# A hybrid attention, recurrence and MLP kernel: thirty input chunks of block 2 by seven products, outputs parked in DRAM

## What is computed

```
h = rms_norm(x, norm_mix)
xa, ga, q, f, v, g, m_a, m_b = split(h @ w_in, 8)          # 1024 x 8192
y_a = rg_lru(conv4(xa), w_r, w_i, lam) * gelu(ga)           # scan over tokens
y_b = rms_norm(hgrn2(silu(q), 1 - f_gate, log f_gate, v)) * silu(g)
y   = sigmoid(m_a) * y_a + sigmoid(m_b) * y_b
x   = x + y @ w_out
x   = x + square(relu(rms_norm(x) @ w_up)) @ w_down         # 4096 wide
return rms_norm(x)
```

## Time and profile before

| | us |
|---|---|
| runs (3) | 3150.05, 3146.99, 3151.70; median 3150.05 |
| profiled execution | 3149.78 |
| its span | 3148.0 |
| busy: PE, DVE, ACT, POOL | 2957.5, 1878.6, 1111.7, 1030.2 |
| granted TensorE clock, mean | 0.976 |

### The profile page before, as it was taken

The page is one execution under the profiler, slowest core; times in us unless marked ns, Lnnn a source line. Parts: engine busy times, 40 slices in busy tenths (PEclk is TensorE's granted clock), DMA queues, the critical chain, the costliest instruction groups (busy, mean ns, idle before and its releaser), DMA issues.

```text
span 3148.0 us, 48352 instructions
## 1 busy us (share of the span) xinstructions
PE 2957.5 (94%) x19622; PEld 1847.6 (59%) x19842; DVE 1878.6 (60%) x3077; ACT 1111.7 (35%) x1972; POOL 1030.2 (33%) x1000
## 2 busy tenths in 40 slices
PE   7979998999979988999999999999999989999998
PEld 7529876884439667864565655655655434444443
DVE  2475797773489996644465465365364474545455
ACT  2353455663356745643231232132232221111111
POOL 1401365000512681012522322323221334545452
PEclk9998999999989999999999999999999999999999
DMA  7323142002201341021211111110112101111111
GB/s 248 133 69 108 58 148 88 15 22 96 96 14 42 110 142 32 12 85 67 82 41 41 41 41 41 54 41 28 54 41 81 41 27 54 54 54 54 54 54 74
DMA packets 49165, 207.13 MB, mean 66 GB/s; under 512 B 4488, under 2 KB 9776, under 8 KB 32304
## 3 DMA queue, kind: packets, MB, share of 16 engines
q1 hardware_dynamic: 42288, 195.63, 18.0%
q10 hardware_dynamic: 6656, 8.39, 0.9%
HBM read 187.22 MB, written 16.79 MB: 65 GB/s over the span
## 4 chain that ended last, share of the span: by engine, by line
PE 75%; DVE 18%; ACT 4%; issue 3%; DMA 0%; SPq 0%; DVEq 0%; ACTq 0%
PE big L276 16%; PE big L277 16%; PE big L275 15%; PE banks L275 5%; PE banks L276 5%; PE banks L277 5%; PE banks L1046 3%; DVE arena L1800 2%; DVE arena L1787 2%; PE banks L917 2%; DVE arena L2034 1%; PE big L591 1%; PE banks L591 1%; DVE arena L2200 1%; DVE arena L2014 1%
## 5 line engine op out<-in xcount | busy, mean ns | idle before, releaser
L561 POOL TENSOR_TENSOR w_lo<-stage,w_hi 128x512 bf16<-128x512 f32 x464 | 588.1, 1299 | 380.6 <-ACT w_hi L1245 380.0
L554 POOL CAST w_hi<-stage 128x512 bf16<-128x512 f32 x376 | 251.1, 709 | 1383.0 <-PE big L277 1188.2
L276 PE MATMUL big<-ht_lo,w_hi 128*128 128x512 bf16 x1161 | 440.0, 379 | 4.3 <-DVE ht_lo L1685 1.8
L277 PE MATMUL big<-ht_hi,w_lo 128*128 128x512 bf16 x1163 | 440.8, 379 | 1.2
L275 PE MATMUL big<-ht_hi,w_hi 128*128 128x512 bf16 x1137 | 430.9, 379 | 11.2 <-DVE arena L2061 6.5
L275 PE MATMUL big<-w_hi,ht_hi 128*128 128x256 bf16 (+1 forms) x1272 | 379.8, 299 | 12.9 <-DVE arena L1618 4.7
L276 PE MATMUL big<-w_lo,ht_hi 128*128 128x256 bf16 (+1 forms) x1274 | 380.3, 298 | 4.0 <-issue 3.7
L277 PE MATMUL big<-w_hi,ht_lo 128*128 128x256 bf16 (+1 forms) x1276 | 380.7, 298 | 0.3
L1800 DVE TENSOR_SCALAR_CACHE_REDUCE arena<-arena,smalli 128x512 bf16<-128x512 f32 (+5 forms) x268 | 206.7, 827 | 2.4
L275 PEld LDWEIGHTS big<-ht_hi,w_hi 128*128 128x128 bf16 x1184 | 117.5, 99 | 148.0 <-issue 11.5
L277 PEld LDWEIGHTS big<-ht_hi,w_lo 128*128 128x128 bf16 x1184 | 115.8, 98 | 139.7
(11 more groups left out here) (361 smaller groups left out, 6598.9 us busy)
## 6 DMA issues: line engine op xcount, KB each, us to landing
stage<-in_w SPq DMA_DIRECT2D x130, 1024.0 KB, 4.8
arena<-in_w_ada SPq DMA_DIRECT2D x48, 512.0 KB, 4.2
arena<-in_x SPq DMA_DIRECT2D x16, 512.0 KB, 7.6
xs<-arena SPq DMA_DIRECT2D x16, 512.0 KB, 2.6
arena<-xs SPq DMA_DIRECT2D x16, 512.0 KB, 8.3
gt<-arena ACTq DMA_DIRECT2D x16, 256.0 KB, 2.5
arena<-gt ACTq DMA_DIRECT2D x16, 256.0 KB, 2.6
out_x<-arena SPq DMA_DIRECT2D x8, 512.0 KB, 2.6
```

Source lines behind the costliest of these rows:

```text
L276: pe.matmul(out, ah, bl, start=False, stop=False)
L277: return pe.matmul(out, al, bh, start=False, stop=stop)
L554: pool.tensor_copy(w_hi[:, n % RING, c0:c1], stage[:, n % RAW_RING, c0:c1]).then_inc(s_w_hi_split, mark(s_w_hi_split, n, q))
L561: ins = pool.tensor_tensor(w_lo[:, n % RING, c0:c1], stage[:, n % RAW_RING, c0:c1], w_hi[:, n % RING, c0:c1], ALU.subtract)
```

## The change

**Block 2 input chunks.** 30 of the 32 (all but xa0 and f0, and not ri) go by seven products of 512 x 512 by 128 quarters. p1, p6, p7 and p4 are added up in one PSUM bank, p5 and p3 in another, p2 in a third. ACT copies the partial sums out after p1, p6 and p5 and applies the function after p4; DVE has three adds. PE waits before p6 for ACT's copy of p1, before p7 for that of p6, before p3 for that of p5, and before p4 for DVE's c22. Chunk order is xa, f, q, v, ri, ga, mb, gg, ma, and one step of the recurrence follows every seventh of 28 groups (four steps in a chunk, four in ri as before).
**Their weights.** POOL makes four sums and seven low parts, ACT seven high parts, for the chunk after the one that PE is in. A chunk has seven parts of 512 columns; two such slots and one for ri take the ring.
**Token sums** of block 2 (`sums_2`) are made by DVE and ACT at its start.
**Outputs** of bands 0 to 2 are stored in DRAM (`y2`), and loaded again by ACT (`y2_load`) after p4 of ma3; `first_two` waits for all six. SP loads six tiles of x after the same product, two after y2_f.
**MLP**: up2 is an ordinary chunk; three adds in place of seven, with partial sums in PSUM and ACT copies; `token_sums(1)` goes beside the first `add_down`, and behind the copy of up1 on ACT.
**Block 1**: the order of `choose` and the convolution on DVE, and the ada pieces spread inside `conv_in`.

```diff
-B_CHUNKS = ["xa", "f", "q", "v", "ri", "ga", "ma", "gg", "mb"]
+B_CHUNKS = ["xa", "f", "q", "v", "ri", "ga", "mb", "gg", "ma"]
-STRASSEN = range(2, 16)
+STRASSEN = range(3, 16)
+SEVEN = [n for n, (l, c) in enumerate(CHUNKS) if l == 2 and c[:-1] in B_CHUNKS and c[:-1] != "ri" and c not in ("xa0", "f0")]
+PRODUCTS = (("p1", 0, "b11", "u"), ("p2", 1, "b21", "p2"), ("p6", 4, "t2", "u"), ("p5", 3, "t1", "p5"), ("p7", 5, "t3", "u"), ("p3", 6, "b22", "p5"), ("p4", 2, "t4", "u"))
...
+        IN_CHUNK = {"v": hsteps[0:4], "ga": hsteps[8:12], "mb": hsteps[12:16], "gg": hsteps[16:20], "ma": hsteps[20:24]}
...
-                if n == CHUNK_AT[(2, "up1")]:
+                if n == CHUNK_AT[(2, "o3")]:
+                    sp.wait_ge(s_gemm, when(s_gemm, "q", "ma", 3, "p4"))
                     for i in range(NT):
+                        if i == 6:
+                            sp.wait_ge(s_hgrn_dve, when(s_hgrn_dve, "y2_f", 3, 1))
...
+                    pool.tensor_tensor(SUM3, a11, a21, ALU.subtract).then_inc(s_sum, mark(s_sum, n, 5))
+                    pool.wait_ge(s_sum, when(s_sum, n, 5))
+                    pool.tensor_tensor(a21, a21, a22, ALU.add).then_inc(s_sum, mark(s_sum, n, 3))
+                    for sem, value in used_by(n) if events else ():
+                        pool.wait_ge(sems[sem], value)
+                    low(0, a11).then_inc(s_sum_lo, mark(s_sum_lo, n, 0))
...
+            def seven(c, b, hgrn=None):
...
+                    if name == "p6":
+                        pe.wait_ge(s_p_out, when(s_p_out, c, b, "u1"))
+                    if name == "p7":
+                        pe.wait_ge(s_p_out, when(s_p_out, c, b, "u2"))
+                    if name == "p3":
+                        pe.wait_ge(s_p_out, when(s_p_out, c, b, "p5"))
+                    if name == "p4":
+                        pe.wait_ge(s_c_out, when(s_c_out, c, b, "c22"))
...
+                            if steps and done % (7 * len(turns_)) == 0:
+                                hgrn(*steps[done // (7 * len(turns_)) - 1])
...
+                copied("u1", "p1", "u", "c11", ACT.Copy, (0, 1, 2), u1)
...
+                copied("u2", "p6", "u", "c12", ACT.Copy, (3, 5, 4), u2)
...
+                copied("p5", "p5", "p5", "c22", ACT.Copy, (6,), p5)
...
+                copied("c21", "p4", "u", "c21", func, None, None)
...
+                seven("ga", b, ACT.Gelu_apprx_tanh, hgrn, u2=roots)
...
+                seven("ma", b, ACT.Sigmoid, hgrn, c21=y2_load if b == 3 else None)
...
+                add("c11", "p2", "p2", "u1", c11)
...
+                add("c22", "p7", "u", "p5", c22)
...
+                add("c12", "p3", "p5", "u2", c12)
...
+                    sums_2(0)
+                    sums_2(1)
+                    conv_2(0, 0)
...
+                    conv_2(0, 1)
+                    seven("q", 0)
+                else:
+                    recurrent(b - 1, 0)
+                    normed_state(b - 1, 1)
+                    seven("xa", b, c11=(lambda: y2_low(b - 1, 0), lambda: gated_state(b - 1, 1)), c22=(lambda: recurrent(b - 1, 1),), c12=(lambda: y2_low(b - 1, 1),))
+                    conv_2(b, 0)
+                    seven("f", b, c11=(lambda: conv_2(b, 1),))
+                    seven("q", b, c11=(lambda: forget(b, 0), lambda: forget(b, 1)))
...
+                seven("ga", b, hgrn, c22=(lambda: scanned(0),), c12=(lambda: scanned(1), pad))
+                seven("mb", b, hgrn, c11=(lambda: normed_state(b, 0),))
+                seven("gg", b, hgrn)
+                seven("ma", b, hgrn, c11=(lambda: gated_state(b, 0),))
...
-                pe.wait_ge(s_hgrn_dve, when(s_hgrn_dve, "y2_lo", 2, 1))
+                pe.wait_ge(s_y2_in, when(s_y2_in))
...
-                choose(3, 0, 1)
                 conv_out(8)
                 conv_out(9)
-                choose(3, 2)
                 conv_out(10)
                 conv_stats()
-                choose(3, 3)
+                choose(3, 0, 1)
                 conv_shift()
-                choose(3, 4)
+                choose(3, 2, 3, 4)
...
-                choose(7, 0, 1)
+                choose(7, 0, 1, 2, 3, 4)
                 gated_convolution(2)
                 gated_convolution(3)
-                choose(7, 2, 3, 4)
```

More of the change, by code:

```diff
@@ L377, in build @@
[L377 to L387, removed]
@@ L1526, in _ @@
+                seven("mb", b, ACT.Sigmoid, hgrn)
+                for m in range(2):
+                    act.wait_ge(s_hgrn_dve, when(s_hgrn_dve, "lvl", b, m, 0))
+                seven("gg", b, ACT.Silu, hgrn)
+                seven("ma", b, ACT.Sigmoid, hgrn, c21=y2_load if b == 3 else None)
+            for m in range(2):
+                y2_high(3, m)
             for i in range(NT):
@@ new lines, in seven, with add @@
+            def seven(c, b, hgrn=None, c11=(), c22=(), c12=()):
+                steps = IN_CHUNK.get(c, [None] * 4)
+                def add(out, p, to, copied, rest):
+                    dve.wait_ge(s_gemm, when(s_gemm, "q", c, b, p))
+                    dve.wait_ge(s_p_out, when(s_p_out, c, b, copied))
+                    dve.tensor_tensor(quarter(c, out), quarter(c, out), product(c, b, to), ALU.add).then_inc(s_c_out, mark(s_c_out, c, b, out))
+                    if to != "u":
+                        freed(s_c_out, "q", c, b, to)
+                    for fn in rest:
+                        fn()
+                if steps[0]:
+                    hgrn(*steps[0])
+                add("c11", "p2", "p2", "u1", c11)
+                if steps[1]:
+                    hgrn(*steps[1])
+                add("c22", "p7", "u", "p5", c22)
+                if steps[2]:
+                    hgrn(*steps[2])
+                add("c12", "p3", "p5", "u2", c12)
+                if steps[3]:
+                    hgrn(*steps[3])
@@ L2268, in quarters @@
-                add("c11", c11, PU[0], "p2")
+                    dve.wait_ge(s_p_out, when(s_p_out, j, copied))
+                    dve.tensor_tensor(out, x, tile(to, "st", j, to), ALU.add).then_inc(s_c_out, mark(s_c_out, j, name))
+                c11, c12, c22 = RT[0][:, 0:512], RT[0][:, 512:1024], RT[1][:, 512:1024]
+                for n in range(2):
+                    dve.wait_ge(s_rs_lo, when(s_rs_lo, j - 1, n))
+                add("c11", c11, PU[0], "p2", "p2", "u1")
                 freed(s_c_out, "st", j, "p2")
-                add("u2", PU[1], PU[0], "p6")
@@ L2407, in pack_2 @@
         if j in STRASSEN:
[L2408 to L2410 removed]
+            quarters(f"up{j}", up)
         else:
```

731 lines of the change are left out of this document (472 added, 259 removed).

## The result

Twenty runs of each kernel: 3156.9 us after (3153.1 to 3160.7), 3152.0 before (3146.9 to 3158.6); ratio 1.0015, interval 1.0008 to 1.0022. So the kernel is 4.9 us longer, a difference that this many runs can tell, but smaller than the 0.2% (6.3 us) that the prediction took as what can hardly be told from no change. The forecast was 3161. The profiled execution has a span of 3156.2 us against 3148.0.

The account below looks back on a forecast made before the run. TensorE, busy 2957.5 us of a 3148.0 us span, was taken as the bound. Terms -6.5 + 17.5 - 15 + 6 + 17 - 9.7 + 2 = +11.3 gave 3161 us, range 3105 to 3195.

Parts of the forecast that it names:

- Forecast A: Whole kernel: the 76 us that PE gains are given back as waits; own range 3145 to 3178 us; chance 0.48.
- the parked tiles: End of block 2: PE waits 17 us for six reloaded tiles, +17; +9 with the whole bandwidth, +20 at 331 GB/s.
- three signs of being wrong: ga below 28 us, PE starting the output GEMM within 10 us, or PE waiting for POOL's w_lo in most chunks.
- rival B: Block 2, faster: DVE and POOL do not meet as laid out; 3104 us in full, between 3104 and 3143; chance 0.36.
- the start: Start of block 2: DVE's 26 token sums and ACT's late copies, +17.5 us, 10 if nothing meets POOL.
- xa to q: Chunks xa, f, q: waits sum to 10 us, 64.4 against 62.3, +2.1 three times, +6.
- C: Chunks without steps (f, q), slower still: POOL's weights are late, 32 us, 3193 us; chance 0.16.
- The reading of mb: mb: reciprocal and multiply behind the add of c11 make level 1 on PE late, 3.5 + 1.7 = 5.2 us.
- The four bands: v to ma in block 2: waits of 14.1 us, 160.0 against 163.8 us, -3.8 four times, -15.
- a term of zero: Block 1's ada pieces: same count, no row shows PE waiting for them, so 0, 2 us if a DMA is late.
- The rest of block 1: Before attention: wait for L2007 falls 1.9 us per layer, conv_stats about 1.5 earlier; -6.5, bounds -10 and 0.
- the MLP's loop: MLP loop: seven waits for L2308 (some 11 us) go, 13 x 1.0 us at down tiles 0 come; +2, between -10 and +8.

Follow-up runs that it names:

- a_narrow: Changed kernel with POOL's low parts of the thirty chunks computed on 32 of 512 columns, four sums kept: 3102.8 us.
- a_recip: Changed kernel with the reciprocal and its multiply at the head of mb on DVE, ahead of the diagonal: 3149.9 us.
- a_five: Changed kernel with five order edits (start of block 2; xa, f, q; mb's reciprocal in quarters; parked-tile loads earlier; MLP's PSUM turn): 3101.3 us, ratio to before 0.9845.
- b_ch: Kernel before with only the new order of choose and the convolution on DVE: span 3147.3 us.
- b_ada: Kernel before with layer 0's sixteen ada pieces one by one behind each quarter of conv_in: 3136.2 us, ratio 0.9953.
- a_six: a_five with ga's second-half DVE operations behind c22, second scan behind mb's c11, second Sqrt moved, q0's high parts earlier on ACT: 3108.1 us, ratio 0.9872.
- half (7): Part of a_six: ACT's high parts of q0's weights ahead of and between the token sums at block 2's start; moved the start by 0.1.

## Why the prediction was right, and where not

**The shape.** Forecast A held: PE's gain in block 2 was given back as waits, and the large ones stand where the prediction put them. ga before p3 4.5 (forecast 4.3), mb before level 1 4.3 (3.5), xa before p4 3.9 (4.7), the parked tiles 16.4 (17), down tiles 0 thirteen times 1.0 (1.0). None of its three signs of being wrong came: ga is 31.8 us, the output GEMM starts 18.3 after p4, and PE waits for POOL's w_lo 3.5 us in all. Timeline of the kernel after, ga's chain and then mb's:

```profile
1835.56 2.18 DVE L2489 TENSOR_TENSOR arena<-arena 128x1024 f32<-128x1024 f32 x1
1836.62 4.22 POOL L587 TENSOR_TENSOR w_lo<-stage,w_hi 128x512 bf16<-128x512 f32 x2
...
1839.87 1.53 DVE L2491 TENSOR_SCALAR arena<-arena 128x1024 f32<-128x1024 f32 x1
1841.43 1.06 ACT L1717 ACTIVATE arena<-arena 128x1024 f32<-128x1024 f32 x1 [5.31 <-DVE arena L2491]
1842.39 0.58 ACT L1587 ACTIVATE arena<-big 128x512 f32<-128x512 f32 x1
1843.02 0.61 PE L282 MATMUL big<-ht_hi,w_hi 128*128 128x512 bf16 x1 [4.50 <-ACT arena L1587]
...
1864.28 6.55 DVE L2385 RECIPROCAL arena<-arena 128x1024 f32<-128x1024 f32 x1
1870.86 1.31 DVE L2386 SCALAR_TENSOR_TENSOR arena<-arena,vec 128x1024 f32<-128x1024 f32 x1
...
1876.22 0.68 PE L1175 MATMUL banks<-arena 128*128 128x64 f32 x3 [4.34 <-DVE arena L2469]
```

DVE ends its eighth operation 18.6 us into ga; 18.2 was forecast beside POOL, 13 alone. a_narrow shows both halves: without most of POOL's work ga is 5 us shorter and the kernel 3102.8 us, while mb stays, priced from the reciprocal alone. That is near the price of rival B in full (3104), but partly by luck: v to ma gave 29 us where B had 36, and the start and xa to q 26 where B had 21. B and C (no chunk of f or q waits long for POOL) did not happen. The reading of mb was right as to what is late and incomplete as to why: the 6.55 us cost PE the wait in both places where they stood in one piece (the kernel after and a_recip), and spread over mb and gg in quarters they cost 0.3 (a_five). Whether being cut or having less ahead of level 0 does it was not told apart. The four bands, priced at -15, measured -15.1.

**The largest miss** is a term of zero. "The ada pieces are the same count; no row shows PE waiting for them, so 0": 18.7 us. The step looked at waits, and there was none; the loss was in the granted clock, which stands at 0.62 to 0.86 in the windows of that stretch before the change, and for which the prediction, whose clock term is one for the time behind a wait (28% of 6.1 us), did not look where PE is busy. Bounds of 0 and +2 held no gain at all.

**The rest of block 1** has the right size (-5.8 against -6.5) and only in part for the reasons given. The prediction had two terms in each layer: 1.9 us off the wait for L2007, and about 1.5 for an earlier `conv_stats`. The wait for L2007 falls from 3.3 to 2.5. The wait ahead of the turned pieces, for ACT's normalised outputs, which is `conv_stats`' part, is in the kernel before

```profile
PE banks L763 <- ACT arena L1340: 7.1, 2, 4.5
```

and 2.5 after (2 times, 1.2 each). A wait that the prediction did not have, for `split_normed` (L1851 before, L2066 after), grows from some 1.2 us in each layer to 3.7. From the end of conv_in to the first products of the attention behind the queries the first layer takes 188.4 us after and 188.5 before; the gain lies in the second, 186.2 against 190.8 from its first transposes on. The order alone (b_ch) does the same, 188.3 and 186.7, and the pieces alone (b_ada) make the first 5.3 longer. So the size is luck in part: in the first layer the order does no more than take back what the pieces lose there.

**The time is right because misses cancel, which is luck.** Against -18.7 stand terms that came out 15.6 longer than forecast: the start 5.8, xa to q 4.5, the MLP's loop 3.0 and start 1.1, the rest of block 1 0.7, the end 0.6, and v to ma 0.1 the other way. In the start the waits were found (11.5 for the copy of xa0 behind t4, 8.0 for that of f0), and their clock was not. The window of xa0 to q0 after:

```profile
1463.96:1552.95 88.99, 68.21 (x308) 31.39 (x309) 74.97 (x60) 32.66 (x44) 45.48 (x28) 0.89 0.12 42
```

The clock is granted at 0.89 there: the 276 matmuls of 512 columns at 0.216 us and the two groups of transposes at 1.74 us would be 63.1 us, and PE is busy 68.2. DVE is busy 75 us: its 26 sums are made at 1.22 us alone and 2.17 beside POOL. f's wait before p4 is 2.4 us, not 0.9: its two convolutions run beside POOL, at 5.6 and 6.4 us for three taps. In the loop of the MLP a down tile 0 costs 1.1 us from start to start, thirteen times (14.4); the waits for L2308 cost 1.57 each, and six of the seven lie in this stage (9.4), so it grows by 5.0. The seventh ends the stage ahead of it, which should have gained it too, and did not because of the 2.8 us for DVE that are left there. Only the bank of p4 was at fault in the loop, as a_five shows (-13.8).

**Two sums of the prediction do not add up as written.** The parts that it lists for the 24 steps are 45.2 us, not 44.1: 23.5 holds the 1.5 in which PE was not busy. The 44.1 is the right one: after the change the chunks without a wait have 6.9 (gg) to 7.7 us (ma) for four steps. And the terms of the parked tiles (2.7, 1.5, and 6.3 MB at 380 GB/s) are 20.8 us, not 18.7. The trace has 18.3 from the end of p4 to the first matmul behind it: the first data (SP's) flow 1.2 us after p4 and the parked tiles' 2.8, not 4.2, and 6.3 MB take 16.4 us, which is 383 GB/s.

**DVE and POOL.** Start of block 2, kernel after:

```profile
1499.06 2.43 DVE L2324 TENSOR_TENSOR arena<-arena 128x1024 bf16<-128x1024 f32 x2
...
1502.75 1.16 POOL L587 TENSOR_TENSOR w_lo<-stage,w_hi 128x512 bf16<-128x512 f32 x1 [16.98 <-ACT w_hi L1573]
...
1505.02 2.17 DVE L2307 TENSOR_TENSOR arena<-arena,ht_lo 128x1024 f32<-128x1024 f32 x1
...
1506.07 2.13 POOL L587 TENSOR_TENSOR w_lo<-stage,w_hi 128x512 bf16<-128x512 f32 x1
```

Unhindered they take 1.2 each; beside each other 2.17 and 2.13, so the two streams together do hardly more than one after the other would (1.22 + 1.16 = 2.4 for a pair, 2.2 between two starts of DVE). The Trainium skill (SBUF — State Buffer, Who interferes with whom) says that a DVE instruction with two inputs in SBUF and a GpSimd instruction that reads SBUF exclude each other for the whole instruction. The trace agrees to within 0.2 us in 2.4. POOL's loss did not reach PE: a chunk's weights have 18 us or more.

**The end.** With the x loads behind, the parked tiles cost 8.8 us, near the +9 forecast for that case; with both at once 16.4. The two queues of the kernel after between 2390 and 2412 us, SP's and ACT's (packets, MB, share):

```profile
q1 hardware_dynamic: 864, 3.15, 36.9%
q10 hardware_dynamic: 864, 3.15, 35.6%
```

Their last data land within 0.3 us of each other. That is sharing. The Trainium skill (DMA: Bandwidth & Descriptors, Queues, rings and completion order) says that each DMA engine goes round-robin between the queue rows that have work, by packets; the trace agrees. The prediction took the place of the loads as given, and so did not see that all six regions are free well before p4. Issued some 14 us earlier (a_five) they cost nothing themselves; ma3 is 16.5 us shorter, and the output GEMM 10.8 longer, for POOL and DVE are then late.

**What stays open.** In xa the wait only moves into f: a_five has 38.5 us of DVE's work in the two (17.8 and 20.7) against 36.3 us of matmuls, and no edit tried takes any away. That DVE's sum is the bound there is argued from these two numbers. a_six's half (7) shows the same for the start. How much of DVE's work would go if its outputs of bands 0 to 2 were not split and stored again was not tried.

## To carry over

A wait names the instruction that came last, not the engine that lacks time: before moving the instruction ahead of it, add up the busy time of each engine in that chunk. If it is below the length that the chunk has without waits, look for the gap into which the long operation fits (or cut it into pieces that fit). If it is not, as in ga (28.5 against 25.9) and xa (23.5 against 18.1), the wait moves until work goes to a chunk that has room, as the second scan did from ga to mb. Read the granted clock of each stage as well as the waits: an engine that is busy all the time can still lose a sixth of it (18.6 of 111.2 us here). And price a term of "nothing" from both sides like any other.

## What the runs showed of the hardware

Sixty-four one-column float32 products in a row (8.7 to 11.2 us) leave PE busy and at a mean granted clock of 0.62 to 0.80 (1.00 is 2.4 GHz), and the 5.8 us of full matmuls behind the first of these groups at 0.71; sixteen at a time (1.7 us) between blocks of 24 matmuls of 256 columns leave it at 0.98. DMA queues of SP and ACT with 3.15 MB each took 16.4 us together (383 GB/s) and held PE up for 16.4 us; with SP's loads behind, ACT's held it up for 8.8. The reciprocal on DVE costs 6.4 to 6.8 ns for each element of a partition (6.55 us for 1024, and 1.75 for 256 in a_five), five times a TENSOR_TENSOR of 1024 (1.2 us).
